# The output projection token tile by token tile, its norms beside it, and the first two FFN slots on token halves

## The reference

```python
h = rmsnorm(x, norm_mix_pre);  proj = h @ w_in                     # 1024 -> 8704 columns
y_a, y_b, y_c = rwkv7(...), short_conv(...), dilated_attention(...)
merged = g_a * (y_a @ wb[:512]) + g_b * (y_b @ wb[512:1024]) + g_c * (y_c @ wb[1024:])
x = x + rmsnorm(merged @ w_out, norm_mix_post)                     # the stage in question
h = rmsnorm(x, norm_ffn_pre)
gate, up = split(h @ w_ffn_in);  x = x + rmsnorm((silu(gate) * up) @ w_ffn_out, norm_ffn_post)
```

## Time and profile before

| | |
|---|---|
| time, median of 3 runs | 1148.91 us (1147.95 to 1149.37) |
| profiled execution | 1148.54 us, of which the span from first to last instruction is 1146.6 us |
| PE busy | 1055.9 us, 92% of the span |
| DVE, ACT, POOL busy | 460.2, 374.6, 447.0 us |
| granted TensorE clock, mean | 0.966 of full |
| DMA | 117.20 MB, 102 GB/s over the span |

### The profile page before, as it was taken

The page is one execution under the profiler, slowest core; times in us unless marked ns, Lnnn a source line. Parts: engine busy times, 40 slices in busy tenths (PEclk is TensorE's granted clock), DMA queues, the critical chain, the costliest instruction groups (busy, mean ns, idle before and its releaser), DMA issues.

```text
span 1146.6 us, 15082 instructions
## 1 busy us (share of the span) xinstructions
PE 1055.9 (92%) x6277; PEld 853.0 (74%) x6277; DVE 460.2 (40%) x550; ACT 374.6 (33%) x483; POOL 447.0 (39%) x343
## 2 busy tenths in 40 slices
PE   3999889999999999999688899959999999999997
PEld 3887778777877877787467487748888888888885
DVE  4013641873386268428735756061122122210003
ACT  5121512351253135122553533272233233221112
POOL 7435421542264235214300236324454554554531
PEclk9999899999999999999789799979999999999998
DMA  6232321242133223425400624603333334223221
GB/s 220 75 110 73 111 93 57 75 146 75 56 111 111 93 72 112 163 96 196 153 1 1 232 81 148 219 15 95 97 86 110 85 98 110 75 108 110 74 74 74
DMA packets 106767, 117.20 MB, mean 102 GB/s; under 512 B 2462, under 2 KB 86492, under 8 KB 106716
## 3 DMA queue, kind: packets, MB, share of 16 engines
q1 hardware_dynamic: 98080, 99.10, 26.9%
q10 hardware_dynamic: 8636, 17.34, 4.0%
HBM read 100.17 MB, written 16.25 MB: 102 GB/s over the span
## 4 chain that ended last, share of the span: by engine, by line
PE 60%; issue 15%; DVE 14%; POOL 5%; ACT 4%; ACTq 1%; DMA 0%; POOLq 0%; DVEq 0%
PE ps L1199 13%; PE ps L1200 13%; PE ps L1201 13%; PE ps L1293 10%; POOL w_lo L529 5%; PE ps L1348 2%; PE ps L1341 2%; DVE sq L920 1%; DVE xm L900 1%; DVE xm L899 1%; PE ps L1326 1%; PE ps L1370 1%; PE ps L1377 1%; DVE xm L898 1%; DVE h_f L839 1%
## 5 line engine op out<-in xcount | busy, mean ns | idle before, releaser
L529 POOL TENSOR_TENSOR w_lo<-w_raw,w_hi 128x512 fp32r<-128x512 f32 x304 | 434.8, 1461 | 669.4 <-ACT w_hi L561 669.0
L561 ACT CAST w_hi<-w_raw 128x2048 fp32r<-128x2048 f32 x76 | 144.9, 1907 | 205.5 <-PE ps L1201 180.0
L1199 PE MATMUL ps<-a_hi,w_hi 128*128 128x512 f32 x512 | 201.6, 394 | 7.6 <-issue 3.8
L1200 PE MATMUL ps<-a_lo,w_hi 128*128 128x512 f32 x512 | 201.1, 393 | 0.0
L1201 PE MATMUL ps<-a_hi,w_lo 128*128 128x512 f32 x512 | 200.9, 392 | 0.0
L1293 PE MATMUL ps<-a_hi,w_hi 128*128 128x512 f32 x384 | 158.4, 412 | 0.0
L1293 PE MATMUL ps<-a_lo,w_hi 128*128 128x512 f32 x384 | 152.9, 398 | 0.0
L1293 PE MATMUL ps<-a_hi,w_lo 128*128 128x512 f32 x384 | 151.9, 396 | 0.0
L1199 PEld LDWEIGHTS ps<-a_hi,w_hi 128*128 128x128 f32 x512 | 97.3, 190 | 28.8 <-issue 8.3
L1200 PEld LDWEIGHTS ps<-a_lo,w_hi 128*128 128x128 f32 x512 | 97.3, 190 | 20.3
L1201 PEld LDWEIGHTS ps<-a_hi,w_lo 128*128 128x128 f32 x512 | 97.2, 190 | 20.3
(11 more groups left out here) (245 smaller groups left out, 1375.5 us busy)
## 6 DMA issues: line engine op xcount, KB each, us to landing
w_raw<-w_in SPq DMA_DIRECT2D x34, 1024.0 KB, 5.2
w_raw<-w_ffn_in SPq DMA_DIRECT2D x44, 512.0 KB, 4.8
spill<-spill_buf ACTq DMA_DIRECT2D x27, 512.0 KB, 2.8
w_raw<-w_ffn_out SPq DMA_DIRECT2D x11, 1024.0 KB, 5.0
w_raw<-w_branch SPq DMA_DIRECT2D x5, 1024.0 KB, 8.7
proj<-spill SPq DMA_DIRECT2D x1, 4608.0 KB, 16.0
g_ab<-spill SPq DMA_DIRECT2D x8, 512.0 KB, 4.8
w_raw<-w_out SPq DMA_DIRECT2D x4, 1024.0 KB, 5.1
```

The lines of the kernel that those rows point to most:

```text
L529: last = g.tensor_tensor(w_lo[:, b, c], w_raw[:, b, c], w_hi[:, b, c].bitcast(F), ALU.subtract)
L561: s.copy(w_hi[:, b], w_raw[:, b]).then_inc(hi_ready, 1)
L1199: t_.matmul(dst, w0, a0, start=first, stop=False)
L1200: t_.matmul(dst, w0, a1, start=False, stop=False)
```

## The change

The slots are the same and their number is the same, but their order, their buffers and PE's order in the projection and the first two FFN slots change.

- **Order of slots.** The first two `w_out` slots (`S_KEPT`) move ahead: 35, 36 are M0, M1; 37, 38 are `w_out` 0 and 1; 39, 40 are M2, M3; 41, 42 are `w_out` 2 and 3.
- **Buffers.** `w_out` 0 and 1 get hi and lo buffers of their own (`kept_hi`, `kept_lo`), so that all four parts of `w_out` are resident at once. `x_in`, `gain_mix`, `h2_tok` and `h2_f32` move in memory.
- **PE.** The projection runs token tile by token tile (`out_part`), all four slots for one tile, and `turn_rows(t-1)` stands behind tile t. The last tile takes its slots in the order 2, 3, 0, 1. Slots 43 and 44 are multiplied on tokens 0 to 255 first (`ffn_half(n, m, 0)`), then on tokens 256 to 511; the last tile's transposes stand between.
- **ACT and DVE.** The norms are written out tile by tile instead of with a lag.

```diff
-    S_MERGE = S_ATT + 1
-    S_OUT = S_MERGE + N_MERGE
-    S_FIN = S_OUT + N_OUT
+    MERGE_SLOT = [S_ATT + 1, S_ATT + 2, S_ATT + 5, S_ATT + 6]
+    S_KEPT = S_ATT + 3
+    S_OUT = S_ATT + 7
+    OUT_SLOT = [S_KEPT, S_KEPT + 1, S_OUT, S_OUT + 1]
+    S_FIN = S_OUT + 2
...
# ScalarE, high(n, loaded, b)
+                if isinstance(n, int) and n in (S_KEPT, S_KEPT + 1):
+                    act.wait_ge(att_merged, KT)
+                    s.copy(kept_hi[:, n - S_KEPT], w_raw[:, b]).then_inc(hi_ready, 1)
+                    return
+                if isinstance(n, int) and n == MERGE_SLOT[2]:
+                    act.wait_ge(slot_used, MERGE_SLOT[0] + 1)
...
# ScalarE, merge stage
-            high(S_ATT + 2, raw_value(S_ATT + 2), (S_ATT + 2) % 2)
+            next_slot(MERGE_SLOT[1])
...
+            next_slot(S_KEPT)
             gates(1)
+            next_slot(S_KEPT + 1)
             for g in range(N_MERGE):
-                high(S_MERGE + g + 2, raw_value(S_MERGE + g + 2), (S_MERGE + g) % 2)
+                if g > 0:
+                    next_slot([MERGE_SLOT[2], MERGE_SLOT[3], S_OUT][g - 1])
                 act.wait_ge(pair_merged, g + 1)
                 s.copy(a_hi[:, 2 * g:2 * g + 2], merged[:, 2 * g:2 * g + 2]).then_inc(merged_ready, 1)
                 if g + 2 < N_MERGE:
                     gates(g + 2)
+            next_slot(S_OUT + 1)
...
# ScalarE, norms
+            for t in range(NT):
+                z_root_of(t, 0)
+                if t > 0:
+                    high_part(t - 1)
+                if t == 2:
+                    next_slot(S_FIN)
+                x1_norm(t)
+                if t == 2:
+                    next_slot(S_FIN + 1)
+            high_part(NT - 1)
...
# VectorE, norms
+            for t in range(NT):
+                add_normed(t, 0, x_in, gain_mix, x1, x1_ready)
+                if t == NT - 1:
+                    low_part(t - 1)
+                next_rstd(t)
+                gained(t)
+                if t != NT - 2:
+                    low_part(t)
...
# TensorE
+            for t in range(NT):
+                if t == 2:
+                    pe.wait_ge(pair_merged, N_MERGE)
+                order = (2, 3, 0, 1) if t == NT - 1 else range(N_OUT)
+                for i, m in enumerate(order):
+                    last = out_part(t, m, i == 0, i == N_OUT - 1)
+                    if t == NT - 1 and m >= 2:
+                        last.then_inc(slot_used, 1)
+                last.then_inc(z_tile_done, 1)
+                if t > 0:
+                    turn_rows(t - 1)
...
+            for n in (S_FIN, S_FIN + 1):
+                pe.wait_ge(lo_ready, n + 1)
+                for m in range(2):
+                    ffn_half(n, m, 0)
+                    if n == S_FIN + 1 and m == 0:
+                        turn_rows(NT - 1)
+            pe.wait_ge(a_lo_ready, NT + N_MERGE + NT)
+            for n in (S_FIN, S_FIN + 1):
+                for m in range(2):
+                    last = ffn_half(n, m, 1)
                 last.then_inc(slot_used, 1)
```

More of the change, by code:

```diff
@@ L446, in _ @@
                     sp.dma_start(g_ab[:, g % 2, br], gate[br][:, 2 * g:2 * g + 2]).then_inc(g_ab_loaded[g % 2], 16)
-            for m in range(N_OUT):
-                par.b = (S_OUT + m) % 2
-                load(S_OUT + m, [(half2(par.b), wo[m])])
+            for m in range(2, N_OUT):
+                par.b = OUT_SLOT[m] % 2
+                load(OUT_SLOT[m], [(half2(par.b), wo[m])])
             sp.wait_ge(slot_used, S_OUT)
@@ L542, in _ @@
                                  pattern=[[-1, 2 * P]], channel_multiplier=HD).then_inc(dist_ready, 1)
-            with pool.Fori(S_REST // 2 + 1, N_SLOTS // 2, 1) as i:
+            for n in range(S_REST // 2 * 2 + 2, S_FIN + 1):
+                low(n, n % 2)
+            with pool.Fori((S_FIN + 1) // 2, N_SLOTS // 2, 1) as i:
                 for b in range(2):
@@ L805, in _ @@
                 if t < NT:
-                    z_root_of(t, 1, N_SLOTS)
+                    z_root_of(t, 1)
                 if t > 0:
@@ L1520, in _ @@
                                          k == 0, k == NJ - 1)
-                last.then_inc(slot_used, 1)
[L1524 to L1548, removed]
@@ L1549, in _, with turn_rows, out_part @@
-            pe.wait_ge(a_lo_ready, NT + N_MERGE + NT)
+                last.then_inc(slot_used, 3 if g == 1 else 1)
+            def turn_rows(t):
+                pe.wait_ge(h_ready, NT + t + 1)
+                for k in range(KT):
+                    last = t_.transpose(ps[:, 2 * t + k // 4, k % 4 * P:(k % 4 + 1) * P], h2_tok[:, t, k * P:(k + 1) * P], ident[:])
+                last.then_inc(turned, 1)
+            def out_part(t, m, first, last_part):
+                n = OUT_SLOT[m]
+                hi, lo = (kept_hi[:, m], kept_lo[:, m]) if m < 2 else (w_hi[:, n % 2], w_lo[:, n % 2])
+                wh, wl = [w.rearrange("p (k c) -> p k c", k=2) for w in (hi, lo)]
+                s_ = slice(t * P, (t + 1) * P)
+                if t == 0:
+                    pe.wait_ge(a_lo_ready, NT + m + 1)
+                    pe.wait_ge(lo_ready, n + 1)
+                for k in range(2):
+                    for half in range(2):
+                        c = slice(half * SEQ, (half + 1) * SEQ)
+                        last = three(ps[:, 2 * t + half], a_hi[:, 2 * m + k, s_], a_lo[:, 2 * m + k, s_], wh[:, k, c], wl[:, k, c],
+                                     first and k == 0, last_part and k == 1)
+                return last
@@ new lines, in ffn_half @@
+            def ffn_half(n, m, half):
+                b = n % 2
+                wh, wl = [w[:, b].rearrange("p (k c) -> p k c", k=KT) for w in (w_hi, w_lo)]
+                c, tok = slice(m * P, (m + 1) * P), slice(half * 2 * P, (half + 1) * 2 * P)
+                for k in range(KT):
+                    last = three(ps[:, 2 * (n - S_FIN) + m, tok], wh[:, k, c], wl[:, k, c], a_hi[:, k, tok], a_lo[:, k, tok],
+                                 k == 0, k == KT - 1)
+                return last
@@ new lines, in _ @@
+            pe.wait_ge(a_lo_ready, NT + N_MERGE + 2)
+            for n in (S_FIN, S_FIN + 1):
+                pe.wait_ge(lo_ready, n + 1)
+                for m in range(2):
[4 more added lines that the diff above has]
+            for n in (S_FIN, S_FIN + 1):
+                for m in range(2):
+                    last = ffn_half(n, m, 1)
+                last.then_inc(slot_used, 1)
```

85 lines of the change are left out of this document (54 added, 31 removed).

## The result

The changed kernel takes 1152.43 us (median of 8 runs, 1151.56 to 1153.36), the kernel before 1148.43 beside it: ratio 1.0038, 95% interval 1.0027 to 1.0048. It is slower by 4.0 us, more than the 0.2% that the forecast took as the least that can be told from no change. The forecast was 1150.5.

What follows compares the result with a forecast made beforehand. PE, busy 1055.9 of 1146.6 us, was taken as the bound. Merge stage + 11.1, projection + 7.2 and end of projection to slot 45 - 16.5 gave + 1.9 with rounding, on 1148.54: 1150.5 us, range 1146 to 1156.

Steps and rivals of the forecast that it cites:

- Merge stage: M2's late cast makes PE stand 10.4 us, restart at lower clock costs 2.6; M3 ends 11.1 us later.
- the second rival: Merge stage: M2's weights come in time and M2 follows M1, all behind it 13.0 us earlier, 1137.5; chance 0.10.
- Tile 0: Projection's first tile: PE stands 5.5 us for slot 42's weights, then the lower clock costs 2.6.
- The first rival: Tile 0: the second clock loss does not come after the 5.5 us stand, 1147.9; chance 0.15.
- Norms behind tiles 1 to 3: Projection: each norm's chain of 7.3 us is hidden behind a tile's 10.9, so no stand there.
- Half slots: Slots 43 and 44: a 256-column matmul takes 0.120 us, 23.0 us in all against 21.8.
- the rival in which the halves make the kernel slower: Slots 43 and 44: load and columns don't overlap at 256 columns, pace 0.227, about + 17.5, 1168; chance 0.12.
- Slot 45: PE stands 2.2 us ahead of slot 45, which starts at 799.6; afterwards the old rhythm, no clock loss.
- Longer remainders: Rival: POOL's remainders of slots 39, 42 and 45 need 7.0 us as DVE works beside, 1153.5; chance 0.13.
- Sum: Whole kernel: merge + 11.1, projection + 7.2, end of projection to slot 45 - 16.5; with rounding + 1.9.
- the range: Whole kernel: 1146 to 1156 us, leaving out the 1137.5 case and the dear end of the slow half slots.
- the side that had 0.42: Whole kernel: the outcome slower, meaning above 1151.2 us, chance 0.42.

Runs made afterwards that it cites:

- e1: Changed kernel with ScalarE's cast for M2 moved ahead of the rounding of pair 0 and the gates of group 2: 1148.97 us.
- e5: Changed kernel with slots reordered (M2 between w_out 0 and 1, M3 before w_out 2), M2's buffers and casts moved, slot 42's ahead of merged pair 3: 1134.72 us.
- e2: Changed kernel with slot 42's cast, the last part of w_out, moved ahead of the wait for merged pair 3 and its rounding: 1145.54 us.
- e3: Changed kernel with slots 43 and 44 multiplied on all 512 tokens at once, after the last tile's transposes: 1160.47 us.
- e4: Changed kernel with slot 45's cast run ahead of slot 43's sigmoid and split in two pieces: 1149.32 us.
- e10: The kernel of e5 run once more without further change, to look at the clock at slot 45: 1134.47 us.
- e7: Kernel before the change, with three extra copies ahead of slot 45's cast in the first FFN pass to make TensorE stand: 1151.14 us.
- e8: Changed kernel run once more, nothing altered, to look at the clock at slot 45: 1152.17 us.
- e9: Changed kernel run yet again, nothing altered, for the same question about the clock at slot 45: 1153.73 us.

## Why the prediction was right, and where it fell short

- **Merge stage: right.** Predicted 10.4 us of stand and 2.6 for the clock, + 11.1 in all; the trace shows 10.12 and + 11.0. That the sum is this close is luck. The gates came at 682.01 rather than 683.4, since pair 0 was merged earlier (its rounding starts at 676.72, not 677.97), though "None of this is moved by the change"; POOL's remainder took 6.89 rather than 6.0; and M2 and M3 together took 25.3 us rather than 24.8. That the cast's place was a cause is shown by e1, and that the order of slots was the other part by e1 and e5. The forecast had put the whole stand down to the cast. It said in brackets that slots 37 and 38 don't set it; that holds as the kernel stands, but they take over once the cast is moved. So the second rival, M2 in time if its cast only ran early, was wrong in its condition too: in e1 M2 still stands 4.53 us.
- **Tile 0: right.** Predicted 5.5 us and a fall of the clock; measured 5.17 and 0.50 in the windows. e2 takes the stand down to 1.70 and keeps the clock up, 6.9 us less. The first rival (no second clock loss) did not come.
- **Norms behind tiles 1 to 3: right.** No row with an idle time at these transposes; the projection took 53.3 us, predicted 53.5.
- **Half slots: right.** 0.120 us was taken between 0.113 and 0.227, and 0.12 was measured. By the Trainium skill's rule on weight loads (TensorE: Matmul & The Clock Gate, Part 3, What overlaps and what doesn't) it would have been about 0.22, an estimate from the page's load time. The trace disagreed at 512 columns, and now does at 256 too: the rival in which the halves make the kernel slower had a chance of 0.12, and fell (e3).
- **Slot 45: half right.** The stand was predicted at 2.2 us and is 2.33. But the step ended with "From there on it is the old rhythm". It was not: the clock fell behind this stand, and slot 45 took 12.8 us instead of the 10.9 that the sum gave it. 1.6 of this 1.9 is the clock, since behind a stand with full clock the slot takes 11.2 (e4, e5, e10); the other 0.3 is the restart itself, and it is also in the 2.6 us at which the prediction priced the clock. I had priced a fall only behind the stands of 5 us and more, since 1.44 and 1.77 us had left no trace. But the kernel before had a row for a stand of this size, behind the projection and eight transposes:

```profile
757.03 1.30 PE L1239 MATMUL ps<-ident,h_tok 128*128 128x128 f32 x8 [2.64 <-ACT h_tok L588]
```

The clock was full up to 757.5 and 0.56 in the next window, and the stand of 3.81 us came only after that. The prediction used this fall for tile 0 ("it fell with shorter stands") and not for slot 45, where it should have had a price. The other 0.7 is small change: POOL's remainders of 43 and 44 took 6.0 us each, so slot 44's first half waited 0.43 us, and the rest lies in hand-overs.

- **Longer remainders:** this rival's 1153.5 is nearer to the measured time than the forecast's 1150.5, but its mechanism came for one slot of three: 6.89 us at slot 39, where it gave 7.0, and 4.92 and 5.45 at 42 and 45.
- **Sum:** + 1.9 predicted, + 4.5 in the profile and + 4.0 in the medians; of the 2.6 that the profile has more, 1.6 is the clock at slot 45, 0.3 the restart there and 0.7 the later start. The outcome lies inside the range, on the side that had 0.42.

## What to carry to other kernels

When loads or weights of a later stage are moved ahead, follow every station they pass: here the matmuls kept their order and their work, but the cast of the next slot slid behind a wait for a DMA in ScalarE's program, and two extra slots stood ahead of it in GpSimd's line. Put each cast where its inputs and its buffer are ready and not behind a wait for something younger; it was worth 6.9 us for one line and 17.7 with the order of slots. And give each stand of TensorE its price at the lower clock as well, also short ones.

## What the hardware showed that I had not expected

The clock fell to the lower level at slot 45's stand of 2.33 to 2.61 us in six profiles: three of the changed kernel, and those of e1, e2 and e7. In e8 and e9 it was low before the stand was over, in the other four after the first matmuls behind it. In the kernel before it fell behind the 2.64 us ahead of 757.03. It cost the changed kernel 1.6 us at slot 45. Behind stands of 1.70 (e2) and 1.77 us it did not fall, nor behind 2.33 us in two profiles of the new order. And GpSimd's remainder of a slot, the same four instructions, took 4.9 us with VectorE idle, 6.9 with VectorE at work for 4.6 of them (slot 39), and 7.8 with VectorE at work for 5.5 (e2).
